# Other places in SBUF for the operands of the matmuls: spaced k tiles, and columns in alternating blocks

## The reference, cut to what matters

```python
h = rmsnorm(x, g_pre_mix) * (1 + scale_m) + shift_m        # (256, 2048)
z = h @ w_in                                               # w_in: 2048 x 11,088
q_lat, kv_lat, k_rope, gq, gk, gv, g_lr, g_og, gate_a, gate_b = split(z)
y_a = mla_branch(...) @ w_branch_a                         # 1024 x 2048
y_b = gla_branch(...) @ w_branch_b                         # 2048 x 2048
merged = sigmoid(gate_a) * y_a + sigmoid(gate_b) * y_b
x = x + gate_m * rmsnorm(merged @ w_mix_out, g_post_mix)
h = rmsnorm(x, g_pre_ffn) * (1 + scale_f) + shift_f
a, val = split(causal_conv3(h @ w_ffn_up))                 # 2048 x 11264
x = x + gate_f * rmsnorm((gelu(a) * val) @ w_ffn_down, g_post_ffn)   # 5632 x 2048
```

## Time and profile before

| | us |
|---|---|
| median of two runs | 1599.15 |
| profiled execution | 1598.98 |
| its span, first to last instruction | 1597.2 |
| TensorE matmul busy in it | 1576.0 |
| VectorE busy | 1119.7 |
| ScalarE busy | 820.7 |
| mean of the DMA traffic | 244 GB/s |

### The profile page before, as it was taken

How to read it: one execution, slowest core, us unless ns; L and a number is a source line. 1 busy time by engine, 2 the same in 40 slices (tenths; PEclk the granted TensorE clock), 3 DMA queues, 4 the chain that set the end, 5 groups by cost and what they waited for, 6 DMA issues and landing times.

```text
span 1597.2 us, 29304 instructions
## 1 busy us (share of the span) xinstructions
PE 1576.0 (99%) x11680; PEld 1482.4 (93%) x11680; DVE 1119.7 (70%) x1276; ACT 820.7 (51%) x1076; POOL 6.0 (0%) x11
## 2 busy tenths in 40 slices
PE   7999999999999999999999999999999999999998
PEld 7999999879999999999889999999999999888886
DVE  5897877887867786877757677777777665544444
ACT  5567776657644543444446454455455454443342
POOL 0000000000000000000000000000000000000000
PEclk9999999999999999999999999999999999999999
DMA  9999988874488887877964777777776665555553
GB/s 368 357 319 353 320 269 258 290 243 156 148 263 275 301 281 243 290 266 261 331 210 128 237 248 238 233 239 240 242 253 213 190 198 198 194 194 185 193 196 135
DMA packets 190647, 389.46 MB, mean 244 GB/s; under 512 B 18386, under 2 KB 31058, under 8 KB 189794
## 3 DMA queue, kind: packets, MB, share of 16 engines
q1 hardware_dynamic: 185666, 370.40, 69.2%
q10 hardware_dynamic: 4898, 17.90, 3.3%
HBM read 386.16 MB, written 2.10 MB: 243 GB/s over the span
## 4 chain that ended last, share of the span: by engine, by line
PE 94%; DVE 3%; ACT 2%; issue 1%; DMA 1%; DVEq 0%; ACTq 0%
PE ps L590 21%; PE ps L594 20%; PE ps L592 20%; PE ps L617 8%; PE ps L619 8%; PE ps L618 8%; PE ps L793 1%; PE ps L542 1%; DVE w_lo L1407 1%; PE ps L733 1%; DMA x_tok<-in_x 1%; PE ps L701 0%; PE ps L815 0%; PE ps L732 0%; PE ps L667 0%
## 5 line engine op out<-in xcount | busy, mean ns | idle before, releaser
L1407 DVE TENSOR_TENSOR w_lo<-raw,w_hi 128x1024 fp32r<-128x1024 f32 x530 | 625.7, 1221 | 421.9 <-ACT w_hi L988 421.0
L988 ACT ACTIVATE w_hi<-raw 128x1024 fp32r<-128x1024 f32 x530 | 533.0, 1053 | 637.9 <-PE ps L594 410.3
L590 PE MATMUL ps<-h2t,w_hi 128*128 128x256 f32 x1408 | 390.1, 277 | 0.7 <-DVE h2t L1831 0.7
L594 PE MATMUL ps<-h2t,w_lo 128*128 128x256 f32 x1408 | 389.0, 276 | 0.0
L592 PE MATMUL ps<-h2t,w_hi 128*128 128x256 f32 x1408 | 389.0, 276 | 0.0
L590 PE MATMUL ps<-ht,w_hi 128*128 128x256 f32 x1104 | 309.7, 281 | 0.0
L592 PE MATMUL ps<-ht,w_hi 128*128 128x256 f32 x1104 | 306.1, 277 | 0.0
L594 PE MATMUL ps<-ht,w_lo 128*128 128x256 f32 x1104 | 306.1, 277 | 0.0
L590 PEld LDWEIGHTS ps<-h2t,w_hi 128*128 128x128 f32 x1408 | 264.3, 188 | 0.9 <-issue 0.9
L594 PEld LDWEIGHTS ps<-h2t,w_lo 128*128 128x128 f32 x1408 | 264.6, 188 | 0.0
L592 PEld LDWEIGHTS ps<-h2t,w_hi 128*128 128x128 f32 x1408 | 264.4, 188 | 0.0
(11 more groups left out here) (283 smaller groups left out, 1994.1 us busy)
## 6 DMA issues: line engine op xcount, KB each, us to landing
raw<-in_w_ffn_up SPq DMA_DIRECT2D x176, 512.0 KB, 4.5
raw<-in_w_in SPq DMA_DIRECT2D x168, 512.0 KB, 5.1
ada<-in_w_ada SPq DMA_DIRECT2D x148, 512.0 KB, 6.4
raw<-in_w_ffn_down SPq DMA_DIRECT2D x88, 512.0 KB, 4.1
raw<-in_w_branch_b SPq DMA_DIRECT2D x32, 512.0 KB, 5.4
raw<-in_w_mix_out SPq DMA_DIRECT2D x32, 512.0 KB, 4.9
ada<-in_w_ada ACTq DMA_DIRECT2D x32, 512.0 KB, 4.1
raw<-in_w_branch_a SPq DMA_DIRECT2D x16, 512.0 KB, 5.5
```

The costliest lines, as they stand in the source:

```text
L590: mm(o, w_hi[:, s, k, cols], moving[:, kt, 0], start=opens, stop=False, skip_group_check=True)
L594: ins = mm(o, w_lo[:, s, k, cols], moving[:, kt, 0], start=False, stop=stop, skip_group_check=True)
L988: A(w_hi[:, slot], raw[:, slot], ACT.Copy).then_inc(hi_done, 1)
L1407: V.tensor_tensor(w_lo[:, slot], raw[:, slot], w_hi[:, slot].bitcast(F32), ALU.subtract)\
```

## The change

`ht` and `h2t` get 28 floats (112 bytes) more from one k tile to the next, `hid` 20 floats (80 bytes). The two parts of a k tile stay 1024 bytes apart. `spacer` becomes 1024 bytes shorter, and tensors placed from 48 KB on are put 2048 bytes higher to make room for the longer `ht`, with two exceptions: `lat_s` is put 1792 bytes higher, which makes it begin at 64 modulo 512, and `x1` 4544 bytes. `ht`, `h2t` and `hid` still begin at 320 modulo 512, and so does `merged`, which keeps its 2048 bytes from tile to tile.

The 256 tokens of `og_s` are stored as alternating blocks of 16 floats (64 bytes): the first 16 tokens, tokens 128 to 143, tokens 16 to 31, and so on; those of `ot` as blocks of 4 floats (16 bytes). The writers put them there and the matmuls read them back in the order of the tokens, by a pattern of two halves with 8 (32) blocks each. For this the writing of `og_s` is in two instructions for each one before, on both engines. No matmul is added or removed, and no operand has another value.

```diff
+STEP, HID_STEP = 28, 20
-        spacer = sb("spacer", [P, 2048 - P], U8)
+        spacer = sb("spacer", [P, 1024 - P], U8)
             assert words * 4 <= size_kb * 1024 and (kb + size_kb) * 1024 <= cap_kb, name
-            with nc.sbuf_tensor(name + "_before", [P, max(kb, 0) * 256 + 8], F32):
+            shift = 0 if kb < 48 else 4544 if name == "x1" else 1792 if name == "lat_s" else 2048
+            with nc.sbuf_tensor(name + "_before", [P, max(kb, 0) * 256 + 8 + shift // 4], F32):
+        def stepped(kb, name, n, step, size_kb):
+            t = at(kb, name, [P, n, 2 * S + step], F32R, size_kb)
+            return t[:, :, 0:2 * S].rearrange("p k (h s) -> p k h s", h=2)
-        ht = at(B + 0, "ht", [P, KT, 2, S], F32R, 32)
+        ht = stepped(B + 0, "ht", KT, STEP, 32)
-        h2t = at(B + 0, "h2t", [P, KT, 2, S], F32R, 32)
-        hid = at(B + 32, "hid", [P, FF // P, 2, S], F32R, 88)
+        h2t = stepped(B + 0, "h2t", KT, STEP, 32)
+        hid = stepped(B + 32, "hid", FF // P, HID_STEP, 88)
+        def in_lines(v, e):
+            return v.rearrange("p (b a e) -> p a b e", a=2, e=e)
+        def og_part(ks, part, a):
+            return og_s[:, ks, part].rearrange("p k (b a e) -> p k a b e", a=2, e=16)[:, :, a]
+            def moved(moving, kt, part):
+                if moving is og_s:
+                    return in_lines(moving[:, kt, part], 16)
+                if moving is ot:
+                    return in_lines(moving[:, kt, part], 4)
+                return moving[:, kt, part]
-                                mm(o, w_hi[:, s, k, cols], moving[:, kt, 0], start=opens, stop=False,
+                                mm(o, w_hi[:, s, k, cols], moved(moving, kt, 0), start=opens, stop=False,
...
-                A(ot[:, h, 0], ps[:, 6, 0:S], ACT.Copy).then_inc(ctx_hi, 1)
+                A(in_lines(ot[:, h, 0], 4), ps[:, 6, 0:S].rearrange("p (a b e) -> p a b e", a=2, e=4), ACT.Copy).then_inc(ctx_hi, 1)
-                    A(og_s[:, 4 * q:4 * q + 4, 0], o_gla[:, 4 * q:4 * q + 4], ACT.Copy).then_inc(og_hi, 1)
+                    ks = slice(4 * q, 4 * q + 4)
+                    A(og_part(ks, 0, 0), o_gla[:, ks, 0:P].rearrange("p k (b e) -> p k b e", e=16), ACT.Copy)
+                    A(og_part(ks, 0, 1), o_gla[:, ks, P:S].rearrange("p k (b e) -> p k b e", e=16), ACT.Copy).then_inc(og_hi, 1)
-                V.tensor_tensor(ot[:, h, 1], ps[:, 6, 0:S], ot[:, h, 0].bitcast(F32), ALU.subtract).then_inc(ctx_lo, 1)
+                V.tensor_tensor(in_lines(ot[:, h, 1], 4), ps[:, 6, 0:S].rearrange("p (a b e) -> p a b e", a=2, e=4),
+                                in_lines(ot[:, h, 0], 4).bitcast(F32), ALU.subtract).then_inc(ctx_lo, 1)
-                    V.tensor_tensor(og_s[:, ks, 1], o_gla[:, ks], og_s[:, ks, 0].bitcast(F32), ALU.subtract)\
-                        .then_inc(og_lo, 1)
+                    for a in range(2):
+                        ins = V.tensor_tensor(og_part(ks, 1, a), o_gla[:, ks, a * P:(a + 1) * P].rearrange("p k (b e) -> p k b e", e=16),
+                                              og_part(ks, 0, a).bitcast(F32), ALU.subtract)
+                    ins.then_inc(og_lo, 1)
```

More of the change, by code:

```diff
@@ L206, in at @@
                 words *= n
-            assert words * 4 <= size_kb * 1024 and (kb + size_kb) * 1024 <= cap_kb, name
-            with nc.sbuf_tensor(name + "_before", [P, max(kb, 0) * 256 + 8], F32):
+            shift = 0 if kb < 48 else 4544 if name == "x1" else 1792 if name == "lat_s" else 2048
+            with nc.sbuf_tensor(name + "_before", [P, max(kb, 0) * 256 + 8 + shift // 4], F32):
                 with nc.sbuf_tensor(name, shape, dt) as t:
@@ L589, in feature_pair @@
                                 stop = last and j == 1 and k == 1
-                                mm(o, w_hi[:, s, k, cols], moving[:, kt, 0], start=opens, stop=False,
+                                mm(o, w_hi[:, s, k, cols], moved(moving, kt, 0), start=opens, stop=False,
                                    skip_group_check=True)
-                                mm(o, w_hi[:, s, k, cols], moving[:, kt, 1], start=False, stop=False,
+                                mm(o, w_hi[:, s, k, cols], moved(moving, kt, 1), start=False, stop=False,
                                    skip_group_check=True)
-                                ins = mm(o, w_lo[:, s, k, cols], moving[:, kt, 0], start=False, stop=stop,
+                                ins = mm(o, w_lo[:, s, k, cols], moved(moving, kt, 0), start=False, stop=stop,
                                          skip_group_check=True)
```

## The result

The changed kernel takes 1644.73 us (two runs, 1644.58 and 1644.88) against 1599.15 before: 1.0285 times the time, 95% interval 1.0241 to 1.0329. The forecast was 1573 us, with a range of 1540 to 1606. The time lies outside the range, on the other side of no change.

A forecast was written before the change was run, and what follows sets the result against it. It took the distances between TensorE's matmuls to bound the kernel. Gains of 4.1 + 9.9 + 10.5 + 1.0 = 25.5 us from 1598.98 us gave 1573 us, with a range of 1540 to 1606.

The forecast's parts named there:

- What bounds the kernel: Whole kernel: TensorE, busy for 1576.0 of 1597.2 us, sets the time by the distance from one matmul to the next.
- The step that failed: Matmuls on `ht` and `h2t`: spacing the tiles brings all to 111.7 ns, gaining 4.1 and 9.9 us.
- The 118 ns rhythm: 618 matmuls seen at 118.3 ns: this rhythm should not last with spaced tiles, a gain of 4.1 us.
- all fall into that rhythm: Rival, 256-column matmuls: each tile may meet a bad relation, 6918 x 5.0 = 34.6 us lost, 1634 us; chance 0.07.
- slow blocks: Rival, `ot` and `og_s` matmuls: each 16-byte jump halves the rate, 41.0 and 20.5 us more, 1636 us; chance 0.07.
- `hid`: 1440 matmuls on `hid` and stationary `ht`: spacing gains 7.3 ns each, 10.5 us, the middle between 0 and 21.0.
- `og_s` and `ot`: 1296 matmuls, with `lat_s`: half of 1.6 ns gained each, 1.0 us; blocks of four floats cost nothing.
- The writers: Writes of `og_s` in halves and of `ot`: cost nothing, at most 1.5 us and 3.3 us.
- Places don't matter: Rival, TensorE's matmuls: rates depend on how the stream started, with a fixed cost per load, 1599 us; chance 0.19.
- The loads too become faster: Rival, all spaced or blocked matmuls: 256 columns at 109.4 ns, 58.6 us gained, 1540 us; chance 0.24.
- the slow end of the reading: Whole kernel: `hid` and the blocks gain nothing and the first term half, about 1590 us.

The follow-up runs named there:

- e1: The changed kernel with only `ht` and `h2t` spaced by 112 bytes more, `hid` spacing and blocks undone, moved base kept: 1635.93 us.
- e6: The kernel before with all activation tensors 64 bytes higher, at 128 modulo 256 like the weights, which stay: 1650.06 us.
- e10: The kernel before with `ht` at 32, `og_s` and `hid` at 224, `h2t` and `merged` at 160 modulo 256; `ot`, `lat_s` left at 64: 1639.85 us.
- e2: The changed kernel with only `hid` spaced, by 80 bytes; other spacing and blocks undone, moved base kept: 1603.49 us.
- e3: The changed kernel with only the blocks of `og_s` (64 bytes) and `ot` (16 bytes), no spacing, moved base kept: 1606.16 us.
- e14: As e3, but with blocks of 64 floats (256 bytes) in both `og_s` and `ot`: 1599.69 us.
- e9: The kernel before with everything 64 bytes higher, weights at 192 and activations at 128 modulo 256: 1599.88 us.
- e13: The kernel before with `ht` and `h2t` spaced by 256 bytes more per tile, tensors from 48 KB on 4096 bytes higher: 1599.69 us.
- e4: As e1, but with 128 bytes more from tile to tile in place of 112: 1623.62 us.
- e12: The kernel before with `merged` and `hid` alone 64 bytes higher, at 128 modulo 256 like the weights, the others at 64: 1595.30 us.
- e5: The kernel before with all activation tensors 128 bytes higher, at 192 modulo 256, the weights left at 128: 1640.99 us.
- e11: The kernel before with `og_s` at 48, `h2t` at 80, `merged` at 144, `hid` at 112 modulo 256; `ht`, `ot`, `lat_s` left at 64: 1625.61 us.

## Why the prediction was wrong, point by point

**What bounds the kernel** was right: TensorE's distances are the time. TensorE's idle time did not grow, so the splits, the waits and the DMA queues had no part in the 45.5 us.

**The step that failed** is the first: "It ends that every tile stands in the same relation to the weights", priced at 111.7 ns by line 693. It took the relation of before for a bad or at best a common one, so that leaving it could only help. It was the only one of the nine places tried at which 113.3 ns prevails. In place of the forecast gain of 4.1 + 9.9 = 14.0 us there is a loss of 34.7 (14.1 ahead of `ot`, 20.6 in `h2t`), three quarters of the 45.5. The spaced tiles go at 118.4 ns (e1), at the upper bound of 118.3 that the text gave; the constant places average 118.8 over the eight others of the table, so the spacing gives about what a place picked blind gives. That the bound fits so well is luck: it was read from another case, a slow stretch at the place of before, and single places go beyond it, up to 119.8 (e6) and 120.0 (e10). The reason given for it, a conflict can't make a load faster than alone, speaks about the lower end only and says nothing about where between the ends the value falls. All moving tensors of before lay at one place modulo 256, so no row of that trace could say whether the place was good: that was a reason to take the middle or the neighbouring rhythm, and a far higher chance for slower than 0.09.

**The 118 ns rhythm** in the earlier trace rows was read as a coupling that spacing would dissolve: 4.1 us of gain. With the tiles spaced, all of `h2t` is slow, the passes that were at 113.3 included. The rival built on the same row, all fall into that rhythm, gave 1634 us for `ht` and `h2t` alone; e1, which has that part alone, measures 1635.9. It was held at 0.07 with the words that nearly every tile would be needed, and nearly every tile is slow. But it had the size rather than the mechanism: by the starts the old rhythm keeps to 117 to 119 ns (607 to 626 us before), the spaced tiles scatter mostly from 113 to 124, and e6 holds 120 almost without a change. The *slow blocks* rival came nearest to the measured 1644.7 with 1636 us, by luck: it sums a loss of 61.5 us where 7.7 is seen and a gain of 24.5 where all is loss.

**`hid`:** 10.5 us of gain were forecast from the middle between 228.9 and 214.3; it is a loss of 3.1 us in `hid`, at 231.8 ns (e2), and of some 1.1 us in the part of `ht` that is stationary, which goes from 229.1 to 231.9 ns by its starts (384 matmuls, within the 14.1 us ahead of `ot`). The text's clause that a rate over 228.9 isn't excluded was left to "the slower rival", and none of the rivals has such a term.

**`og_s` and `ot`:** 1.0 us of gain forecast, 7.7 us of loss (6.0 and 1.7 in the stages, e3 the same). The rival that reading in blocks is slow had the sign but the wrong cause and size: 61.5 us by a halved rate for each jump. A jump of 256 bytes is free (e14). `lat_s` was right to be small: it went from 64 to 64 modulo 256. The clause that TensorE reads 64 or 16 bytes in a row and then jumps named what changed, but not what costs.

**The writers** cost nothing on the path, as forecast; in halves they take 685 ns on VectorE and 614 and 617 on ScalarE (groups by form, after), where 688 and 634 were taken from the earlier trace rows:

```profile
L1809 DVE TENSOR_TENSOR og_s<-o_gla,og_s 128x512 fp32r<-128x512 f32 x8 | 5.1, 685 | 0.0
...
L1276 ACT ACTIVATE og_s<-o_gla 128x512 fp32r<-128x512 f32 x4 | 2.5, 617 | 0.0
L1275 ACT ACTIVATE og_s<-o_gla 128x512 fp32r<-128x512 f32 x4 | 2.5, 614 | 0.0
```

**Places don't matter** (0.19) is refuted by e6 to e9: three places at which `h2t` is never at 113.3, and e9, in which the activations of e6's place are. The Trainium skill (SBUF — State Buffer, Who interferes with whom) says that TensorE's two read ports are independent and that it never waits for anyone. Here the distance of the same instruction at the same clock goes from 113.3 to 119.8 ns with nothing but the address changed (before against e6). So for float32r the rule can't be taken to mean that places don't matter; at which port or memory the time goes, no run shows. **The loads too become faster** (0.24): no place gave a 256-column distance under 113.3.

**Small slips in the sum.** "About 1590" for the slow end of the reading comes out at 1587 (1598.98 less 9.9 and half of 4.1). The 618 matmuls of the slow rhythm are those of three stretches alone; by the starts the trace before has some 1060 of 256 columns with 116 to 119 ns. Neither changes the account.

**What stays open.** That two reads meet in the same part of the memory is the natural account, since the difference of the addresses counts (e9), and 256 bytes more change nothing (e13) while 128 do (e4). No run shows the collision itself. Nor is it shown why passes at the good place go at 118 ns at times: before has them in `ht` and in the first `h2t` pass, and `lat_s`, at 113 ns in before, e2 and e13, is at 117 in e3, e9, e12 and e14 with the same relation to the weights. And place 192 has the same two rates, with the shares the other way round (e5, one run). So it seems that the relation to the weights sets which rates a stream can have, and something else, not found, picks between them. Whether the slow rate would prevail at 192 in every run is not known. Nor is it shown why place 112 is as good as 128 for `hid`. Whether the columns meet the load of the next operand, as I take it, or something else that moves with the weights, was not tried apart.

## What to carry to other kernels

In this kernel, with TensorE fed back to back in float32r, the place of the moving operand against the stationary one modulo 256 bytes is worth 4 to 6% of the 256-column matmuls and up to 3% of the 512-column ones. Other kernels were not tried. In one like it: scan the place with one constant shift per run, for each shape by itself, and keep it the same for every tile (pad by multiples of 256 bytes), since varying it averages over places that are mostly bad here. Expect some passes at a second rate even at the best place. A trace in which all operands have one place tells nothing about the others; an even distance near the ideal there may be the good case already.

## What the runs showed of the hardware that was not expected

- The good place is narrow: 16 bytes to either side of it cost 5.9 to 6.1 ns of 113.3 (e11). The place as far from the weights on the other side (192) has both 113.3 and 117.8 (e5).
- The two shapes want different places: at place 128 the 256-column matmuls are at 119.8 and the 512-column ones at 226.7, both the extreme or near it in opposite directions (e6); at 64 it is 113.3 and 228.9.
- One relation to the weights can have two rhythms, 113.3 and 118 ns, at the same clock, and a stream keeps one for many passes (`lat_s` in before against e9, `h2t` within before and within e5).
- In the changed kernel the distance wavers from one matmul to the next (0.11 to 0.13 us), while the sum over a stretch repeats from kernel to kernel to the count: `h2t` after and in e1 has 357 matmuls in 42 us, and the kernel before, e2, e3, e9, e12, e13 and e14 all have 373.
